# Weight blocks laid side by side for four products, tokens read last to first for two

## The chip, the cores and the metric

The kernel runs on one core of a Trainium2 chip, as one launch. The metric is the device time of that launch in microseconds (us), lower is better; two runs of the kernel before stand at 2233.84 and 2236.26 us, median 2235.05 us. Layouts of the inputs are made on the host ahead of the launch and are not in the time.

## The reference

512 tokens of 1024 features go through two blocks. The first is a gated recurrence and a gated linear attention side by side, then a feed-forward net (FFN 1). The second is a retention layer with FFN 2, then a sparse-attention layer with FFN 3. What matters here are the large products, each a token matrix against a weight matrix:

```python
# first block, D_MODEL = 1024, D_FF = 2816
h = rms_norm(x, norm1[l]);  p = h @ w_in[l]                     # w_in_t (17 tiles), w_in_v
x = x + mix                                                      # mix = ... @ w_out[l]
h = rms_norm(x, norm2[l]);  gate, up = jnp.split(h @ w_ffn_in[l], 2, axis=-1)   # ffn1_in (44 tiles)
x = x + (jax.nn.silu(gate) * up) @ w_ffn_out[l]                  # ffn1_out
return rms_norm(x, final_norm)
...
# second block, for layer 0 (retention) and layer 1 (sparse attention)
normed = rms_norm_2(h, mix_norm_pre[layer])
proj = x @ w_in                       # retention: ret_t (32 tiles), ret_v; attention: kv_t, kv_v, nsa_t
h = h + rms_norm_2(mixed, mix_norm_post[layer])
normed = rms_norm_2(h, ffn_norm_pre[layer])
h = h + rms_norm_2(swiglu_ffn(normed, ffn_w_in[layer], ffn_w_out[layer]), ffn_norm_post[layer])  # ffn2, ffn3
```

The comments name the kernel's own products.

## The kernel before

**Layout.** Activations lie with features on the 128 partitions: XT, AH and AL are [128, 8, 512], eight feature blocks of 512 tokens. A product is computed in tiles of 128 output features by 512 tokens. Each float32 operand is split in two float32r parts, a high one (AH, WH) and the rest (AL, WL), and every block of 128 input features takes three matrix multiplications: high by high, high weight by low activation, low weight by high activation. `part` (matmul line L379) issues one such block. The weight block, 128 x 128, is the stationary operand, which TensorE loads column by column ahead of the multiplication; the activation block, 128 x 512, is the moving operand, which streams through. So each matmul has a weight load of its own, even where the same WH block serves two in a row. A tile of a product with 1024 input features is 8 blocks, 24 loads and 24 matmuls of 512 columns. `tokens` (L427) does the products that are wanted with tokens on partitions; there the activations are the stationary operand and the weights move.

**Weights.** `Plan` lists all weights in the order of use, in units of [128, 1024] (8 blocks of 128 columns, in the host layout made by `feature_tiles`). For each unit SyncE starts one transfer into one of three RAW buffers, ScalarE rounds it into WH (L827), VectorE takes the rest into WL (L1254), and TensorE waits for both. The three buffers of each kind keep this some units ahead. In WH and WL the 128 columns of block k are elements 128 k to 128 k + 127 of each partition: one run.

**Activations.** `high` (ScalarE, L837) writes AH = XT times a gain, `low` (VectorE, L1272) writes AL = XT times the gain less AH. Their key `st` names the product that follows: "a" (w_in), "f1" (FFN 1), "f2", "kv", "q", "f3" (FFN 3); the retention's own are written at L1079 and L1603.

**Order of work.** Every engine has a program written out by hand, with semaphores between them. `three` opens a product: for each feature block as it becomes ready it runs the block of three output tiles, while the norm of the layer before is being applied block by block (for FFN 3: L1585 scale, L1592 add to the stream, L837 high, L1272 low). `fourth` runs the fourth tile with the sums for the norm (L444, L478) in between, `tile` all the others. Results of ffn_in leave PSUM at L1311 with the norm's factor from RS, which has one number for each token, in ascending order of tokens, and the gate (L1040, L1557, L1045, L1559) writes HH and HLO, the operands of ffn_out.

**Strided readers elsewhere.** L1746 copies windows of CK for the attention's compression with an inner step of 16 elements (64 bytes). L1805 adds a bias row read from last to first (inner step of minus one element). L478 spreads one column over 128 (its stationary operand is one column of `rstok`, `rso` or `small`, read 128 times, inner step 0).

Of the kernel before, what the change touches and what calls it, by code (L numbers as in the profile page):

```python
# [10 lines left out]
ACT = mybir.ActivationFunctionType  # L11
ALU = mybir.AluOpType
AX_X = mybir.AxisListType.X

S = 512
# [6 lines left out]
W_SLOTS = 3  # L22
# [11 lines left out]
for _name, _w in VEC_NAMES:  # L34
    VEC_AT[_name] = _n
    _n += _w
NVEC = _n

K_TILES = {"w_in_t": 8, "w_out": 8, "ffn1_in": 8, "ffn1_out": 22, "ret_t": 8, "ret_out": 16, "ffn2_in": 8,
           "ffn2_out": 22, "kv_t": 8, "nsa_t": 8, "nsa_out": 8, "ffn3_in": 8, "ffn3_out": 22}  # L40

# [104 lines left out]
def build(nc, D, out):  # L146
    p = plan()
    n_units = len(p.units)
    with ExitStack() as ctx:
# [6 lines left out]
        XT = sb("XT", [128, 8, S])  # L156
        AH = sb("AH", [128, 8, S], F32R)
        AL = sb("AL", [128, 8, S], F32R)
# [15 lines left out]
        BANK = [ctx.enter_context(nc.psum_tensor(f"bank{i}", [128, 512], F32)) for i in range(8)]  # L174
# [84 lines left out]
        w_high, x_high, squared, rooted = (signal(n) for n in ("w_high", "x_high", "squared", "rooted"))  # L259
        free_a, lru_a, gla_a, gate_a, hid_a, ret_a, kv_a, exped, turned = (  # L260
            signal(n) for n in ("free_a", "lru_a", "gla_a", "gate_a", "hid_a", "ret_a", "kv_a", "exped", "turned"))
        w_low, x_low, added, inverse, stream = (signal(n) for n in ("w_low", "x_low", "added", "inverse", "stream"))
# [13 lines left out]
        def V(name, i=0, n=1):  # L276
            at = VEC_AT[name] + i
            return vec[:, at:at + n]
# [12 lines left out]
        TURN, MIX = 3, 6  # L291
        A_GROUP = len(STEPS) // 4

        def cols(i, br):
            return 7 + 8 * i if br == 0 else 128 * (i + 1)

# [57 lines left out]
        def tensor_program(e):  # L354
            tenant = {}

            def enter(b, key):
# [2 lines left out]
                    e.wait_ge(*freed(tenant[b]))  # L360
                tenant[b] = key

            def part(name, m, kk, x, ready=None, passes=(0, 1, 2)):
                kt, k, u = K_TILES[name], kk % 8, p.first[name, m] + kk // 8
                b, w, sl = p.bank[name, m], u % W_SLOTS, slice(k * 128, (k + 1) * 128)
                for n in passes:
                    if n == 0:
                        if kk == 0:
                            enter(b, (name, m))
                        if k == 0:  # L370
                            e.wait_ge(*w_high.at(u))
                        if ready:
                            e.wait_ge(*ready[0](kk))
                    elif n == 1 and ready:
                        e.wait_ge(*ready[1](kk))
                    elif n == 2 and k == 0:
                        e.wait_ge(*w_low.at(u))
                    wt, xx = (WH[w], x[0]) if n == 0 else (WH[w], x[1]) if n == 1 else (WL[w], x[0])
                    t = e.matmul(BANK[b][:, :], wt[:, sl], xx[:, kk, :], start=kk == 0 and n == 0,  # L379
                                 stop=kk == kt - 1 and n == 2)  # L380
                    if n == 2 and kk == kt - 1:
                        t.then_inc(matmul.did(("unit", u), (name, m)))
                    elif n == 2 and k == 7:
                        t.then_inc(matmul.did(("unit", u)))
# [143 lines left out]
            for f in range(2):  # L528
                enter(6 + f, ("kt", f))
                e.wait_ge(*gla_v.at(("k", f)))  # L530
                for tt in range(4):
                    t = e.transpose(BANK[6 + f][:, ROWS[tt]], KG[:, f, ROWS[tt]], ident[:, :])
# [92 lines left out]
            for h in range(4):  # L625
# [21 lines left out]
                for j in range(4):  # L647
                    n = S - 128 * j
                    b = p.bank["scores", h, j]
# [4 lines left out]
                    for d in range(2):  # L654
                        t = e.matmul(BANK[b][:, 0:n], KR[:, d, j * 128:(j + 1) * 128], QR[:, d, j * 128:S],  # L655
                                     start=d == 0, stop=d == 1)
                    t.then_inc(matmul.did(("scores", h, j)))
                tile("ret_t", 8 * h + 4, A)
                for j in range(4):
                    e.wait_ge(*free_v.at(("scores", h, j)))  # L660
                    e.wait_ge(*free_a.at(("ret_v", h, j)))
                    for et in range(4):
                        if j == 0:
                            enter(4 + et, ("or", h, et))
                        t = e.matmul(BANK[4 + et][:, j * 128:S], VR[:, j, et * 128:(et + 1) * 128], ST[j][:, :],  # L665
                                     start=j == 0, stop=j == 3)
# [61 lines left out]
            for tt in range(4):  # L728
                t = e.transpose(BANK[6][:, 48 * tt:48 * tt + 48], T[3][0:48, ROWS[tt]], ident[0:48, 0:48])
# [66 lines left out]
            for f in range(8):  # L796
                b = 2 + f % 4
# [3 lines left out]
                for i in range(4):  # L801
                    t = e.transpose(BANK[b][:, ROWS[i]], OT[:, i, f * 128:(f + 1) * 128], ident[:, :])
# [12 lines left out]
        def scalar_program(e):  # L815
# [18 lines left out]
                    ahead(p.first[name, c] + q + LOOK)  # L834

            def high(st, f, gain):
                e.activation(AH[:, f, :], XT[:, f, :], ACT.Copy, scale=V(gain, f)).then_inc(x_high.did((st, f)))  # L837

            def square_for_pair(st, f):
                if f > 1:  # L840
# [92 lines left out]
            for f in range(2):  # L933
                e.wait_ge(*gla_v.at(("bc", f)))
                e.activation(DG[:, f, :], BC[:, f, :].rearrange("p (c t) -> p c t", t=64)[:, :, 63], ACT.Exp,
                             scale=1.0 / 16).then_inc(gla_a.did(("decay", f)))
# [12 lines left out]
            for tt in range(4):  # L949
                e.wait_ge(*matmul.at(("w_in_v", 0, tt)))  # L950
                if tt == 0:
                    e.wait_ge(*inverse.at("a"))
                e.activation(VG[:, tt, :], BANK[p.bank["w_in_v", 0, tt]][:, :], ACT.Copy,
                             scale=rstok[:, tt:tt + 1]).then_inc(free_a.did(("w_in_v", 0, tt)))
# [121 lines left out]
            for f in range(8):  # L1076
# [5 lines left out]
                if f > 2:  # L1082
                    e.wait_ge(*added.at(("gained", f - 2)))
                e.activation(SQ2[f % 2][:, :] if f else SUM2[:, :], XT[:, f, :], ACT.Square,
                             scale=V("final_norm", f)).then_inc(squared.did(("gained", f)))
# [158 lines left out]
        def vector_program(e):  # L1244
# [24 lines left out]

            def low(st, f, gain):  # L1270
                e.wait_ge(*x_high.at((st, f)))
                e.scalar_tensor_tensor(AL[:, f, :], XT[:, f, :], V(gain, f), AH[:, f, :], ALU.mult,  # L1272
                                       ALU.subtract).then_inc(x_low.did((st, f)))

            def add_pair(st, q):
                e.wait_ge(*squared.at((st, 2 * q + 1)))
# [640 lines left out]
    return np.ascontiguousarray(w.reshape(k // 128, 128, m // 128, 128).transpose(2, 1, 0, 3).reshape(m // 128, 128, k))  # L1917


def token_tiles(w):  # L1920

    k, m = w.shape
    return np.ascontiguousarray(w.reshape(8, 128, m // 512, 512).transpose(2, 1, 0, 3).reshape(m // 512, 128, 4096))
# [21 lines left out]
def laid_out(inp):  # L1945
# [24 lines left out]
    w = a["w_in"][0]  # L1970
# [27 lines left out]
    w2 = [a[n].reshape(2, 128, 64).transpose(1, 0, 2) for n in ("cmp_w2_k_2", "cmp_w2_v_2")]  # L1998
    w2 = np.stack(w2, axis=1)
    d["cmp_w2"] = np.concatenate([w2, w2], axis=3)  # L2000
    return {k: np.ascontiguousarray(v) for k, v in d.items()}


# [13 lines left out]
```

## Time and profile before

| | |
|---|---|
| runs, median | 2233.84 and 2236.26 us, 2235.05 us |
| profiled execution, own time | 2235.35 us |
| its span, first to last instruction | 2233.6 us |
| mean granted TensorE clock | 0.976 of full |
| PE busy | 2156.9 us, 97% |
| PE weight loads busy | 1774.0 us, 79% |
| VectorE, ScalarE busy | 1043.8 us (47%), 855.1 us (38%) |

PE is TensorE's matmuls, PEld its weight loads, DVE is VectorE, ACT is ScalarE. Matmuls are pipelined: the length of one record (389 ns) reaches over the start of the next, so the busy share says little about the rate, and the distance from one start to the next is the cost of one.

### The profile page before, as it was taken

The numbers are of one execution on the slowest core, as the hardware profiler recorded it, in microseconds if no ns is written. First come the engines' busy times: TensorE is split into PE (matmuls) and PEld (weight loads), VectorE is DVE, ScalarE is ACT, GpSimd is POOL, SyncE is SP. The second block draws the span as 40 slices with busy tenths as digits, with TensorE's granted clock in tenths as the row PEclk, the third lists the DMA queues.
The fourth block names the chain that finished last, engine by engine and source line by source line (L and its number), as shares of the span: only waits on it lengthen the run. The fifth ranks groups of instructions, "written<-read, shape, count | busy, mean of one in ns | idle before, by whom it ended". The sixth has DMA issues, their size and how long they took to land.

```text
span 2233.6 us, 26303 instructions
## 1 busy us (share of the span) xinstructions
PE 2156.9 (97%) x10252; PEld 1774.0 (79%) x10252; DVE 1043.8 (47%) x1939; ACT 855.1 (38%) x1466; POOL 12.7 (1%) x24
## 2 busy tenths in 40 slices
PE   7899999999999999999999999899999999999997
PEld 6677788888878778787888888777888977888886
DVE  5546444434345345334544422564666736444323
ACT  4563333323313323333333322344767744333221
POOL 0000000000000000000000000000000000000000
PEclk9899999999999999999999999999989999999998
DMA  4212333333322222131333333422010022333331
GB/s 132 74 57 76 95 100 98 94 92 93 106 81 77 70 90 85 57 104 57 104 99 100 92 95 93 148 78 85 30 32 18 1 85 66 95 100 98 87 94 64
DMA packets 51818, 184.44 MB, mean 83 GB/s; under 512 B 5818, under 2 KB 6090, under 8 KB 51440
## 3 DMA queue, kind: packets, MB, share of 16 engines
q1 hardware_dynamic: 49248, 171.99, 24.7%
q0 software_dynamic: 2160, 10.63, 1.4%
q8 instruction: 82, 1.34, 0.2%
q14 instruction: 40, 0.33, 0.0%
q10 hardware_dynamic: 288, 0.15, 0.0%
HBM read 180.61 MB, written 2.14 MB: 82 GB/s over the span
## 4 chain that ended last, share of the span: by engine, by line
PE 89%; DVE 5%; ACT 4%; issue 2%; DMA 0%; SPq 0%; DVEq 0%; ACTq 0%
PE bank L379 69%; PE bank L427 6%; PE bank L782 3%; PE bank L762 2%; PE bank L665 1%; DVE WL L1254 1%; PE bank L753 1%; PE bank L776 1%; PE bank L752 1%; PE bank L478 1%; PE bank L655 1%; ACT WH L827 1%; PE bank L444 1%; DVE MF L1585 0%; DMA RAW<-in_w_in_t 0%
## 5 line engine op out<-in xcount | busy, mean ns | idle before, releaser
L379 PE MATMUL bank<-AH,WH 128*128 128x512 f32 x1648 | 654.5, 401 | 22.4 <-ACT AH L837 15.4
L1254 DVE TENSOR_TENSOR WL<-RAW,WH 128x1024 fp32r<-128x1024 f32 (+1 forms) x326 | 391.4, 1205 | 592.9 <-ACT WH L827 592.2
L379 PE MATMUL bank<-AL,WH 128*128 128x512 f32 x1648 | 645.1, 395 | 3.5 <-DVE AL L1272 3.5
L379 PE MATMUL bank<-AH,WL 128*128 128x512 f32 x1648 | 642.2, 394 | 2.4 <-DVE WL L1254 2.4
L827 ACT ACTIVATE WH<-RAW 128x1024 fp32r<-128x1024 f32 (+1 forms) x326 | 338.1, 1041 | 592.4 <-PE bank L379 510.9
L379 PEld LDWEIGHTS bank<-AH,WH 128*128 128x128 f32 x1648 | 313.8, 191 | 93.9 <-issue 20.8
L379 PEld LDWEIGHTS bank<-AL,WH 128*128 128x128 f32 x1648 | 313.6, 191 | 71.9 <-DVE AL L1272 9.7
L379 PEld LDWEIGHTS bank<-AH,WL 128*128 128x128 f32 x1648 | 313.5, 190 | 69.7 <-DVE WL L1254 3.7
L379 PE MATMUL bank<-HH,WL 128*128 128x512 f32 x528 | 208.6, 395 | 0.0
L379 PE MATMUL bank<-HH,WH 128*128 128x512 f32 x528 | 208.6, 395 | 0.0
L379 PE MATMUL bank<-HLO,WH 128*128 128x512 f32 x528 | 208.5, 395 | 0.0
L1311 DVE TENSOR_TENSOR T<-bank,RS 128x512 f32<-128x512 f32 x156 | 106.5, 686 | 162.0 <-PE bank L379 162.0
L379 PEld LDWEIGHTS bank<-HLO,WH 128*128 128x128 f32 x528 | 99.1, 188 | 24.1
L379 PEld LDWEIGHTS bank<-HH,WH 128*128 128x128 f32 x528 | 99.1, 188 | 24.1
L379 PEld LDWEIGHTS bank<-HH,WL 128*128 128x128 f32 x528 | 99.1, 188 | 24.0
L1040 ACT ACTIVATE T<-T 128x512 f32<-128x512 f32 x66 | 41.7, 631 | 127.2 <-DVE T L1311 127.2
L1045 ACT ACTIVATE HH<-T 128x512 fp32r<-128x512 f32 x66 | 41.7, 632 | 125.8 <-DVE T L1557 125.8
L427 PE MATMUL bank<-WH,AH 128*128 128x512 f32 x192 | 77.1, 402 | 5.9 <-DVE XP L1311 3.6
L427 PE MATMUL bank<-WL,AH 128*128 128x512 f32 x192 | 76.9, 401 | 1.6 <-DVE WL L1254 1.6
L427 PE MATMUL bank<-WH,AL 128*128 128x512 f32 x192 | 76.8, 400 | 0.0
L782 PEld LDWEIGHTS bank<-VS,PT 128*128 128x128 f32 x480 | 68.3, 201 | 1.5
L782 PE MATMUL bank<-VS,PT 128*128 128x64 f32 x480 | 68.1, 275 | 0.0
(285 smaller groups left out, 2309.6 us busy)
## 6 DMA issues: line engine op xcount, KB each, us to landing
RAW<-in_ffn_in SPq DMA_DIRECT2D x132, 512.0 KB, 3.5
RAW<-in_ffn_out SPq DMA_DIRECT2D x48, 512.0 KB, 3.5
RAW<-in_ret_t SPq DMA_DIRECT2D x32, 512.0 KB, 3.5
RAW<-in_ffn_out SPq DMA_DIRECT2D x24, 384.0 KB, 3.1
RAW<-in_w_in_t SPq DMA_DIRECT2D x17, 512.0 KB, 3.7
RAW<-in_ret_v SPq DMA_DIRECT2D x16, 512.0 KB, 3.6
RAW<-in_ret_out SPq DMA_DIRECT2D x16, 512.0 KB, 3.6
RAW<-in_nsa_t SPq DMA_DIRECT2D x9, 512.0 KB, 3.5
```

The lines of the kernel that those rows point to most:

```text
L379: t = e.matmul(BANK[b][:, :], wt[:, sl], xx[:, kk, :], start=kk == 0 and n == 0, stop=kk == kt - 1 and n == 2)
L427: t = e.matmul(BANK[b][:, :], xx[:, kk, tt * 128:(tt + 1) * 128], wt[:, sl], start=kk == 0 and n == 0, stop=kk == 7 and n == 2)
L444: t = e.matmul(BANK[4][:, 4 * tt + q:4 * tt + q + 1], SQ[1][:, ROWS[tt]], ones[:, :], start=True, stop=True)
L478: t = e.matmul(BANK[5][:, ROWS[tt]], src[:, at + tt:at + tt + 1].broadcast_to([128, 128]), ident[:, :], start=True, stop=True)
L655: t = e.matmul(BANK[b][:, 0:n], KR[:, d, j * 128:(j + 1) * 128], QR[:, d, j * 128:S], start=d == 0, stop=d == 1)
L762: t = e.transpose(BANK[b][0:k, j * 128:(j + 1) * 128], SS[s % NSS][:, j * 128:j * 128 + k], ident[:, :])
L782: t = e.matmul(BANK[b][:, 64 * br:64 * br + 64], PT[s % NPT][:, j * 128:(j + 1) * 128], VS[:, j, c:c + 64], start=j == 0, stop=j == i)
L827: e.activation(WH[v % W_SLOTS][:, 0:n], RAW[v % RAW_SLOTS][:, 0:n], ACT.Copy).then_inc(w_high.did(v))
L1040: e.activation(a[:, :], a[:, :], ACT.Silu).then_inc(gate_a.did((n, j)))
L1045: e.activation(HH[n][:, j, :], T[2 * (j % 2)][:, :], ACT.Copy).then_inc(hid_a.did((n, j)))
L1254: e.tensor_tensor(WL[w][:, 0:n], RAW[r][:, 0:n], WH[w][:, 0:n], ALU.subtract).then_inc(w_low.did(v))
L1311: e.tensor_tensor(dst, BANK[p.bank[name, m]][:, :], RS[:, :], ALU.mult).then_inc(free_v.did((name, m)))
```

## The change

Two things change, and no instruction is added, removed or moved: on each engine the same operations stand in the same order, on the same tiles, with other access patterns.

**Side by side.** For ffn2_in and ffn3_in two, for ret_t four and for w_in_t eight neighbouring blocks of 128 columns are interleaved column by column on the host (`side_by_side`): column j of the r blocks lie next to each other. The transfer, the rounding (L827) and the remainder (L1254) work on whole units and read and write them in one run as before. The weight load of block k reads 128 elements with a step of r elements, from element (k // r) * 128 r + k % r: steps of 8, 16 and 32 bytes for r = 2, 4 and 8. The other products, ffn1_in among them, keep blocks of one run.

**Backward.** For FFN 1 and FFN 3, `high` writes AH from the last token to the first, `low` reads AH and writes AL that way, and `part` reads AH and AL with an inner step of minus one element as the moving operand of ffn1_in and ffn3_in. Token order in PSUM is as before, so nothing behind it changes.

```diff
+BESIDE = {"ffn2_in": 2, "ffn3_in": 2, "ret_t": 4, "w_in_t": 8}
+BACKWARD = ("f1", "f3")
...
+        def backward(t):
+            return bass.AP(t.tensor, t.offset + S - 1, [t.ap[0], [-1, S]])
+
+        def tokens_of(st, t):
+            return backward(t) if st in BACKWARD else t
...
+            def block(wt, name, k):
+
+                r = BESIDE.get(name, 1)
+                whole = wt[:, :]
+                return bass.AP(whole.tensor, whole.offset + (k // r) * 128 * r + k % r, [whole.ap[0], [r, 128]])
+
             def part(name, m, kk, x, ready=None, passes=(0, 1, 2)):
...
-                b, w, sl = p.bank[name, m], u % W_SLOTS, slice(k * 128, (k + 1) * 128)
+                b, w = p.bank[name, m], u % W_SLOTS
...
-                    t = e.matmul(BANK[b][:, :], wt[:, sl], xx[:, kk, :], start=kk == 0 and n == 0,
+                    t = e.matmul(BANK[b][:, :], block(wt, name, k), backward(xx[:, kk, :]) if name in ("ffn1_in", "ffn3_in") else xx[:, kk, :],
+                                 start=kk == 0 and n == 0,
                                  stop=kk == kt - 1 and n == 2)
...
             def high(st, f, gain):
-                e.activation(AH[:, f, :], XT[:, f, :], ACT.Copy, scale=V(gain, f)).then_inc(x_high.did((st, f)))
+                e.activation(tokens_of(st, AH[:, f, :]), XT[:, f, :], ACT.Copy, scale=V(gain, f)).then_inc(
+                    x_high.did((st, f)))
...
-                e.scalar_tensor_tensor(AL[:, f, :], XT[:, f, :], V(gain, f), AH[:, f, :], ALU.mult,
-                                       ALU.subtract).then_inc(x_low.did((st, f)))
+                e.scalar_tensor_tensor(tokens_of(st, AL[:, f, :]), XT[:, f, :], V(gain, f),
+                                       tokens_of(st, AH[:, f, :]), ALU.mult, ALU.subtract).then_inc(x_low.did((st, f)))
...
+def side_by_side(t, name):
+
+    r = BESIDE[name]
+    m, _, k = t.shape
+    t = t.reshape(m, 128, k // (128 * r), r, 128)
+    return np.ascontiguousarray(t.transpose(0, 1, 2, 4, 3).reshape(m, 128, k))
...
+    for name in BESIDE:
+        d[name] = side_by_side(d[name], name)
```

How many matmuls each part touches (tiles x 8 blocks x 3):

| product | tiles | matmuls | weight step | tokens |
|---|---|---|---|---|
| w_in_t | 17 | 408 | 8 | forward |
| ffn1_in | 44 | 1056 | 1 | backward |
| ret_t | 32 | 768 | 4 | forward |
| ffn2_in | 44 | 1056 | 2 | forward |
| ffn3_in | 44 | 1056 | 2 | backward |

## Rows read from the trace of the kernel before

**Rows 1.** The page: busy time, and the chain that ended last.
```profile
PE 2156.9 (97%) x10252; PEld 1774.0 (79%) x10252; DVE 1043.8 (47%) x1939; ACT 855.1 (38%) x1466; POOL 12.7 (1%) x24
PEclk9899999999999999999999999999989999999998
PE 89%; DVE 5%; ACT 4%; issue 2%; DMA 0%; SPq 0%; DVEq 0%; ACTq 0%
```
**Rows 2.** Busy time of L379 in three stretches: ffn2_in, ffn3_in, ffn1_out.
```profile
core 0: us, PE busy (x) PEld busy (x), PEclk, DMA share, GB/s
1080.00:1280.00 200.00, 200.00 (x884) 165.60 (x883) 1.00 0.31 97
1880.00:2080.00 200.00, 200.00 (x884) 165.62 (x883) 1.00 0.33 98
480.00:600.00 120.00, 120.00 (x516) 96.51 (x515) 1.00 0.33 94
```
**Rows 3.** Timeline in ffn1_in; columns start, length (us), engine, line.
```profile
299.97 0.39 PE L379 MATMUL bank<-AH,WH 128*128 128x512 f32 x1
299.97 0.19 PEld L379 LDWEIGHTS bank<-AL,WH 128*128 128x128 f32 x1
300.20 0.39 PE L379 MATMUL bank<-AL,WH 128*128 128x512 f32 x1
300.20 0.19 PEld L379 LDWEIGHTS bank<-AH,WL 128*128 128x128 f32 x1
300.42 0.39 PE L379 MATMUL bank<-AH,WL 128*128 128x512 f32 x1
```
**Rows 4.** Timeline of PE at half the granted clock, opening of ffn2_in.
```profile
1040.63 0.63 PE L379 MATMUL bank<-AH,WH 128*128 128x512 f32 x1
1041.06 0.63 PE L379 MATMUL bank<-AL,WH 128*128 128x512 f32 x1
1041.49 0.63 PE L379 MATMUL bank<-AH,WL 128*128 128x512 f32 x1
```
**Rows 5.** Short matmuls back to back: busy time of L699 (124 columns each).
```profile
1516.00:1520.00 4.00, 4.00 (x38) 4.00 (x37) 1.00 0.43 133
```
**Rows 6.** Timeline where the next load is L478's, one column read 128 times.
```profile
933.66 0.39 PE L379 MATMUL bank<-AH,WH 128*128 128x512 f32 x1
933.89 0.39 PE L379 MATMUL bank<-AL,WH 128*128 128x512 f32 x1
934.12 0.39 PE L379 MATMUL bank<-AH,WL 128*128 128x512 f32 x1
934.12 0.75 PEld L478 LDWEIGHTS bank<-ident,rso 128*128 128x128 f32 x5
934.34 0.61 PE L478 MATMUL bank<-ident,rso 128*128 128x128 f32 x4
```
**Rows 7.** Groups by shape on VectorE and ScalarE.
```profile
L1272 DVE SCALAR_TENSOR_TENSOR AL<-XT,vec,AH 128x512 fp32r<-128x512 f32 x48 | 35.3, 747 | 13.5 <-ACT AH L837 12.7
L837 ACT ACTIVATE AH<-XT,vec 128x512 fp32r<-128x512 f32 x48 | 33.7, 717 | 40.5 <-DVE XT L1592 25.5 <-DVE XT L1523 14.6
L1805 DVE CUSTOM_DVE_ANT_0 SQ<-bank,TT 128x512 f32<-128x512 f32 x32 | 22.1, 691 | 15.0 <-PE bank L753 14.9
L1746 DVE COPY X<-CK 64x496 f32<-64x496 f32 x16 | 9.8, 612 | 1.0 <-PE bank L699 0.5
L1305 DVE COPY RS<-bank 128x512 f32<-128x512 f32 x5 | 3.5, 691 | 13.5 <-PE bank L478 13.5
```
**Rows 8.** The chain that ended last, in time, at the opening of FFN 3.
```profile
1841.38 0.70 DVE XT L1592
1842.08 0.02 issue
1842.11 0.73 ACT AH L837
...
1853.16 0.67 DVE AL L1272
...
1858.82 0.67 DVE AL L1272
```

## What I expect, written before the changed kernel ran

> **What bounds the kernel now.** I read the page first. TensorE is busy for 97% of the span and makes up 89% of the chain that ended last [rows 1]: the time is, nearly all of it, the number of matmuls times the distance between their starts. Nothing in this change alters the number. So the one question is whether a weight load that reads with a step, or a moving operand read from its end, changes that distance, and everything else is small.
>
> So the second view is the busy time by stretch, used as a counter. In ffn2_in 884 matmuls of 512 columns fit in 200 us, and as many in ffn3_in: 200 / 884 = 0.2262 us each (up to two that reach over the edges are counted too; less those it is 200 / 882 = 0.2267) [rows 2]. In ffn1_out the same shape takes 120 / 516 = 0.2326 us. The granted clock is full, 2.4 GHz, in all three stretches. 512 columns at one column a cycle are 213.3 ns at that clock, so 13.3 ns of each distance, 6%, are something else. ffn1_out differs from the ffn_in products only in where its operands lie (HH and HLO for AH and AL), yet pays 6.4 ns more: where the operands lie can be felt, at the size of a few nanoseconds.
>
> The third view is the timeline. Each weight load starts with the matmul before it and is recorded for 0.19 us, inside the 0.227 us of that matmul: it is hidden [rows 3]. At the half clock (1.2 GHz) the same matmuls start 0.43 us apart, which is 512 columns at 1.2 GHz and nothing over [rows 4]. So the 13 ns are not a fixed price of a matmul; they appear only where columns are asked for at 2.4 GHz. That looks like a limit of what the operand memory delivers, and it is the reason to take the change seriously: an access pattern is what such a limit would depend on.
>
> **The change, part by part.**
>
> *Loads with a step: 2112 matmuls with step 2 (ffn2_in, ffn3_in), 768 with step 4 (ret_t), 408 with step 8 (w_in_t); 3288 in all.* No row of this trace shows a strided weight load. I bound it by neighbours.
>
> How much longer may a load get before anyone notices? L699's matmuls are short (124 columns, 0.05 us of streaming at full clock for each pass), so there loads follow one another as fast as they can: 38 loads and matmuls touch a stretch of 4 us, and with some two cut at the edges that is 4.0 / 36 = 0.111 us from one to the next [rows 5]. That is the true occupancy of a load; the recorded 0.19 us holds its latency too. Against a distance of 0.2267 us the cover is 0.115 us: a load may take twice as long (0.222 us) and still be hidden, by 4 ns.
>
> Does a step slow a reader at this pace? A load takes 128 columns in 0.111 us, 0.87 ns each. The nearest rows are VectorE's. The copy L1746 reads with a step of 64 bytes, twice the largest step of the change: 496 elements in 612 ns. The plain copy L1305 takes 691 ns for 512. Per element that is 1.23 and 1.35 ns, so the strided one pays nothing that one can see [rows 7]. VectorE is another reader, but its pace (about 1 ns an element) is close to a load's. So I take 0 for the length of the load, with the cover as a second reason.
>
> Does a load with a step disturb the stream beside it? From below: where the load beside the stream reads one single column 128 times (L478), the smallest stretch of memory a load can touch, the next start still comes 0.22 us after (934.12 to 934.34), the same as between plain ones [rows 6]. So a load that touches less gives nothing back, and the 13 ns are not paid for the memory that a load touches. That speaks for 0 also where it touches more. The bounds stay wide. Above: ffn1_out's 6.4 ns for operands that lie less well, times 3288 = +21 us. Below: the floor of 213.3 ns, -13.4 x 3288 = -44 us, if the new pattern freed the stream altogether, for which no row speaks. I take 0.
>
> The Trainium skill has a rule against this part. "SBUF — State Buffer", section "SBUF: two separate sides", says that the memory has lines of 16 bytes and that at least two successive accesses to a line are needed for full bandwidth; "Advanced Engine Details and Errata", section "Memory Cachelines", says the same. By it step 2 (8 bytes, two columns a line) is free and steps 4 and 8 (one column a line) are penalised, and the backward read (four tokens a line) is free. The row of L1746, with one element a line and no penalty, disagrees for VectorE. By the rule taken as a doubling of 1176 loads the sum would still be 0, since twice 0.111 us is hidden.
>
> *Backward moving operand: 2112 matmuls (ffn1_in, ffn3_in).* No row shows TensorE reading backward. L1805 on VectorE reads its second operand with a step of minus one: 691 ns for 512 columns, as the forward copy [rows 7]. So direction costs nothing there. But TensorE reads 2.4 elements a nanosecond, over twice VectorE's rate, so the row decides less here than I would like. Above: if reading backward held the stream to half pace, the distance would be that of the half clock, 0.4267 us [rows 4]. Nearer above: 6.4 ns x 2112 = +14 us, the price of place. Below: -13.4 x 2112 = -28 us. I take 0, the row of the only backward reader.
>
> *ScalarE and VectorE: 16 writes of AH and 16 of AL (717 and 747 ns each) turn backward.* [rows 7] For FFN 1 they lie behind a tile of w_out each (24 matmuls, 5.4 us), which hides even a doubling. For FFN 3 the opening chain runs through one L837 and two L1272 (0.73, 0.67, 0.67 us) [rows 8]: 0 if backward writes go at the old pace, +2.1 us if each doubles. L1805 says 0. The rounding of weights (L827, L1254) and the transfers work on runs as before: 0.
>
> **The sum.** 0 + 0 + 0 against the profiled execution's own 2235.35 us, which lies 0.3 us over the median of the runs. I forecast 2236 us, no change. The terms' own bounds near the rows (+21, +14, +2) reach 2272; below I leave some 13 us for a part of the stream's surplus. A measurement of this kernel tells about 2% (45 us) from no change.
>
> **The rivals.**
>
> *1. The stepped load takes from the stream (slower, 12%).* Suppose the surplus of 13.3 ns is the load's reading from the same memory as the stream after all, and grows with the stretch over which the 128 columns are spread: two, four and eight times 13.3 ns. Then +13.3 ns x 2112 = +28 us, +40 x 768 = +31 us, +93 x 408 = +38 us: +97 us, 2332 us. It decides (passes 2%) when it is about half as strong. For it: the surplus exists, it vanishes at the half clock, and it moves with the place of the operands. Against it: the one-column load of rows 6, which touches the least and saves nothing. By the Trainium skill's 16-byte line ("SBUF — State Buffer", as above) the growth would end at step 4, since a column then has a line to itself; the sum by it would be +28 +31 +16 = +75 us, an estimate.
>
> *2. The backward stream runs at half pace (slower, 10%).* A reader that must deliver 2.4 elements a nanosecond may do it by fetching ascending neighbours together. Backward it would fall to one at a time: (0.4267 - 0.2267) x 2112 = +422 us, 2658 us; a loss of 10% of the pace is enough to pass 2% (0.0227 x 2112 = 48 us). For it: the stream is the one reader here that is already at a limit. Against: L1805. The skill's rule, with four accesses to a line either way, sides against this rival too; no run so far shows it.
>
> *3. The load outgrows its cover (slower, 6%).* If steps 4 and 8 make a load three times as long (0.333 us), the load becomes the bound in ret_t and w_in_t: (0.333 - 0.2267) x 1176 = +125 us, 2360 us; four times, (0.444 - 0.2267) x 1176 = +256 us. It decides where a load passes twice its length. This is the direction of the skill's rule, and L1746 is against it.
>
> *4. The new patterns lift the surplus (faster, 4%).* The distance falls to 213.3 ns wherever a pattern changes: 4344 matmuls (3288 + 1056 of ffn1_in) x 13.4 ns = -58 us, 2177 us. For it is only that ffn1_in and ffn1_out differ by place. For a gain of over 2% three quarters of it must come.
>
> That the change does not do what it says I give nothing: host layout and read pattern fit together, and the engines' programs are the same in order and tiles.
>
> **How the numbers follow.** No effect 68%, rivals 12, 10, 6 and 4%. The predicted time is that of no effect, 2236 us; its own range is 2222 to 2272. To hold eight in ten the range goes on to rival 1 with its upper end, 2335 us; rivals 2 to 4 (20%) stay outside. Slower by over 2% is 12 + 10 + 6 = 28%, faster 4%, within 2% 68%.
>
> **What would show it.** In the profile after, the same count over 1080 to 1280 us shows step 2 alone; ffn1_in shows direction alone; ffn3_in shows both; ret_t step 4; w_in_t step 8, in the stretches between its waits. 0.2267 in all five proves the forecast; a longer distance in ffn1_in proves rival 2, one that grows from ffn2_in to ret_t to w_in_t rival 1; matmuls that begin to wait for loads, with weight loads recorded for 0.3 us or more and only in ret_t and w_in_t, rival 3. Loads recorded for longer than 0.19 us with the distance kept would show that a step costs and the cover holds. L837 and L1272 at 717 and 747 ns test the small term. What would make me wrong is, most of all, that VectorE's rows don't carry over to a reader at 2.4 elements a nanosecond.

## The result, and the profile of the changed kernel

The changed kernel takes 2268.6 us (2266.74 and 2270.46), against 2235.05 us: a ratio of 1.0147, 95% interval 1.0122 to 1.0171. It is slower by 33.5 us, clear of the scatter and inside 2%. The profiled execution is the one of 2270.46 us, its span 2268.7 us.

The page of the changed kernel, for [rows 1]. The lines of the code have moved by 16 to 18 (`part` is L395, L444 is `tokens`, L854 is `high`, L1290 is `low`).

```profile
PE 2193.8 (97%) x10252; PEld 1852.9 (82%) x10252; DVE 1043.9 (46%) x1939; ACT 854.8 (38%) x1466; POOL 12.7 (1%) x24
PEclk9889999999999999999999999999989999999998
PE 90%; DVE 5%; ACT 3%; issue 1%; DMA 0%; SPq 0%; DVEq 0%; ACTq 0%
```

VectorE and ScalarE have the same busy time to 0.3 us. Weight loads have 79 us more. The chain that ended last is TensorE's as before.

Where the time went shows best when both profiles are cut at the same places in the work. First the kernel before, then the changed one: the opening with w_in and w_out, ffn1_in, the retention, ffn2_in, ffn3_in. Columns: stretch, its length, busy time and count for each engine (PE, PEld, DVE, ACT, POOL), granted clock as a share of full, DMA share, GB/s.

```profile
0.00:231.00 231.00, 206.46 (x957) 163.12 (x958) 124.35 (x197) 118.23 (x151) 4.28 (x10) 0.96 0.27 86
231.00:477.00 246.00, 243.41 (x1082) 200.75 (x1081) 110.88 (x134) 77.36 (x92) 0.00 (x0) 1.00 0.31 96
...
600.00:940.50 340.50, 338.19 (x1493) 269.67 (x1492) 144.38 (x199) 109.21 (x142) 3.81 (x7) 0.98 0.25 79
...
1038.90:1287.40 248.50, 247.28 (x1096) 203.71 (x1097) 124.50 (x156) 83.39 (x103) 0.00 (x0) 0.99 0.29 91
...
1843.00:2092.00 249.00, 247.83 (x1096) 204.08 (x1097) 124.45 (x156) 83.34 (x103) 0.00 (x0) 0.99 0.30 90
```

```profile
0.00:240.30 240.30, 216.00 (x957) 188.19 (x958) 124.55 (x197) 118.23 (x151) 4.29 (x10) 0.94 0.25 83
240.30:492.70 252.40, 249.86 (x1081) 200.82 (x1080) 110.81 (x133) 77.21 (x92) 0.00 (x0) 1.00 0.29 94
...
615.40:963.00 347.60, 346.23 (x1494) 306.42 (x1493) 144.82 (x199) 109.25 (x142) 3.81 (x7) 0.98 0.23 78
...
1061.30:1316.30 255.00, 253.95 (x1096) 209.34 (x1097) 124.43 (x156) 83.31 (x103) 0.00 (x0) 0.99 0.28 89
...
1872.10:2127.90 255.80, 254.82 (x1096) 213.86 (x1097) 124.44 (x156) 83.38 (x103) 0.00 (x0) 0.99 0.27 88
```

The differences are +9.3 us (opening, steps of 8), +6.4 (ffn1_in, backward), +7.1 (retention, steps of 4), +6.5 (ffn2_in, steps of 2) and +6.8 (ffn3_in, both), 36.1 in all. The stretches in between give back 1.0, and the span is 35.1 us longer. So each touched stretch pays 6.4 to 9.3 us, for quite different edits and for 408 to 1056 touched matmuls.

The opening also ran longer at the half clock: its granted clock is 0.94 for 0.96, and of its 408 w_in_t matmuls 31 start 426 or 427 ns after the one before, where 20 did in the kernel before. Eleven matmuls at 427 ns in place of 245 are 2.0 us of its 9.3, an estimate from these starts. The run of the steps alone (below) shows 0.94 in its opening as well. Why the clock stayed low for longer there is not shown.

The count of matmuls by stretch, for [rows 2]: ffn1_in, ffn2_in, ffn3_in, ffn1_out, and 30 us of ret_t; the first and the last hold a wait each.

```profile
260.00:460.00 200.00, 197.43 (x844) 158.36 (x844) 1.00 0.30 98
1100.00:1300.00 200.00, 200.00 (x858) 165.42 (x858) 1.00 0.30 97
1920.00:2120.00 200.00, 200.00 (x859) 168.86 (x858) 1.00 0.28 93
500.00:600.00 100.00, 100.00 (x432) 81.09 (x431) 1.00 0.30 93
870.00:900.00 30.00, 29.35 (x125) 29.06 (x125) 1.00 0.29 97
```

200 us hold 858 matmuls where they held 884: 0.2333 us from start to start, for 0.2267. From here on, a distance is the mean time from the start of one matmul to the next, at full clock and without waits (under 0.26 us), over a whole product of the profiled execution. ffn1_in, ffn2_in and ffn3_in are at 233.3 to 233.4 ns, ret_t at 235.3 ns, w_in_t at 244.7 ns (before 226.8 to 226.9, then 227.5 and 227.8, which have short stretches between waits). The three ffn_out products, which were not touched, went from 233.3 to 232.4 ns.

The loads themselves, from the view of one source line, in ffn2_in (step 2), ffn3_in (step 2, backward stream), ret_t (step 4), w_in_t (step 8) and ffn1_in (step 1); the three numbers are the shortest, the middle and the longest in ns.

```profile
L395 PEld LDWEIGHTS bank<-AH,WH x286: 193/193/193, 1099.8 to 1299.3; 128*128 128x128 f32 x143
...
L395 PEld LDWEIGHTS bank<-AH,WH x286: 197/197/197, 1919.9 to 2119.4; 128*128 128x128 f32 x143
...
L395 PEld LDWEIGHTS bank<-AH,WL x42: 308/310/311, 869.8 to 899.7; 128*128 128x128 f32 x42
...
L395 PEld LDWEIGHTS bank<-AL,WH x24: 315/331/342, 39.9 to 59.1; 128*128 128x128 f32 x24
...
L395 PEld LDWEIGHTS bank<-AL,WH x282: 188/188/192, 263.3 to 459.9; 128*128 128x128 f32 x141
```

The recorded load takes 188 ns for one run, 193 to 197 for step 2, 310 for step 4, 331 for step 8. The jump, 113 to 117 ns, lies between a step of 8 bytes and one of 16.

And where no stream of 512 columns runs ahead of a load, the longer load shows at once. The timeline of the changed kernel after L495 (the short matmuls of the norm), in ret_t:

```profile
703.71 0.94 PE L495 MATMUL bank<-ident,rso 128*128 128x128 f32 x7
704.41 0.60 PE L395 MATMUL bank<-AH,WH 128*128 128x512 f32 x1
704.86 0.40 PE L395 MATMUL bank<-AL,WH 128*128 128x512 f32 x1
705.09 0.40 PE L395 MATMUL bank<-AH,WL 128*128 128x512 f32 x1
```

The second L395 starts 0.45 us after the first. The same place before (timeline of PE in the kernel before):

```profile
689.05 0.48 PE L379 MATMUL bank<-AH,WH 128*128 128x512 f32 x1
689.37 0.39 PE L379 MATMUL bank<-AL,WH 128*128 128x512 f32 x1
```

There it was 0.32 us. The 0.13 us more are about the growth of the recorded load, 310 ns for 188.

### The profile page after: what moved, and what is told of

Its sections match the earlier page's. It is cut to its first block, busy times and chain, and to the rows that moved or that the text cites. A ratio compares the mean times of both kernels' runs of the same rounds, so it can differ in the third digit from the quotient of the medians.

```text
span 2268.7 us, 26303 instructions
## 1 busy us (share of the span) xinstructions
PE 2193.8 (97%) x10252; PEld 1852.9 (82%) x10252; DVE 1043.9 (46%) x1939; ACT 854.8 (38%) x1466; POOL 12.7 (1%) x24
## 4 chain that ended last, share of the span: by engine, by line
PE 90%; DVE 5%; ACT 3%; issue 1%; DMA 0%; SPq 0%; DVEq 0%; ACTq 0%
PE bank L395 71%; PE bank L444 6%; PE bank L799 3%; PE bank L779 2%; PE bank L682 1%; PE bank L770 1%; DVE WL L1272 1%; PE bank L793 1%; PE bank L769 1%; PE bank L495 1%; PE bank L672 1%; ACT WH L844 1%; PE bank L461 1%; PE bank L578 0%; DMA RAW<-in_w_in_t 0%
## 5 line engine op out<-in xcount | busy, mean ns | idle before, releaser
L395 PE MATMUL bank<-AH,WH 128*128 128x512 f32 x1648 | 671.0, 411 | 22.7 <-ACT AH L854 16.6
L395 PE MATMUL bank<-AL,WH 128*128 128x512 f32 x1648 | 658.6, 403 | 3.0 <-DVE AL L1290 2.9
L395 PE MATMUL bank<-AH,WL 128*128 128x512 f32 x1648 | 654.9, 402 | 0.9 <-DVE WL L1272 0.9
L395 PEld LDWEIGHTS bank<-AH,WH 128*128 128x128 f32 x1648 | 366.3, 223 | 82.7 <-issue 20.3
L395 PEld LDWEIGHTS bank<-AL,WH 128*128 128x128 f32 x1648 | 367.1, 223 | 59.4 <-DVE AL L1290 9.3
L395 PEld LDWEIGHTS bank<-AH,WL 128*128 128x128 f32 x1648 | 366.8, 223 | 54.6 <-DVE WL L1272 1.8
L395 PE MATMUL bank<-HH,WL 128*128 128x512 f32 x528 | 208.3, 395 | 0.0
L395 PE MATMUL bank<-HH,WH 128*128 128x512 f32 x528 | 208.3, 395 | 0.0
L395 PE MATMUL bank<-HLO,WH 128*128 128x512 f32 x528 | 208.3, 395 | 0.0
L395 PEld LDWEIGHTS bank<-HH,WL 128*128 128x128 f32 x528 | 99.5, 188 | 23.3
L395 PEld LDWEIGHTS bank<-HH,WH 128*128 128x128 f32 x528 | 99.5, 188 | 23.2
L395 PEld LDWEIGHTS bank<-HLO,WH 128*128 128x128 f32 x528 | 99.5, 188 | 23.1
L444 PE MATMUL bank<-WH,AH 128*128 128x512 f32 x192 | 76.9, 401 | 6.6 <-DVE XP L1329 4.4
L444 PE MATMUL bank<-WL,AH 128*128 128x512 f32 x192 | 76.5, 398 | 1.6 <-DVE WL L1272 1.6
L444 PE MATMUL bank<-WH,AL 128*128 128x512 f32 x192 | 76.3, 397 | 0.0
```

The lines of the kernel that those rows point to most:

```text
L395: t = e.matmul(BANK[b][:, :], block(wt, name, k), backward(xx[:, kk, :]) if name in ("ffn1_in", "ffn3_in") else xx[:, kk, :], start=kk == ...
L444: t = e.matmul(BANK[b][:, :], xx[:, kk, tt * 128:(tt + 1) * 128], wt[:, sl], start=kk == 0 and n == 0, stop=kk == 7 and n == 2)
```

## The experiments

After the first look two theories stood. **Meeting:** TensorE's stream and the load beside it read the same memory, and the distance depends on how the two walks through it meet, which is place, step and direction together; on top of that a step of 16 bytes or more makes the load itself long. **Pattern price:** each departure from a forward run has its fixed price, wherever the operands lie.

**Steps moved to other products.**

```diff
-BESIDE = {"ffn2_in": 2, "ffn3_in": 2, "ret_t": 4, "w_in_t": 8}
-BACKWARD = ("f1", "f3")
+BESIDE = {"ffn1_in": 4, "ffn2_in": 8, "ffn3_in": 4, "ret_t": 2}
+BACKWARD = ("f3",)
```

> The steps change places among the products: step 4 for ffn1_in (forward), step 8 for ffn2_in (forward), step 4 with backward tokens for ffn3_in, step 2 for ret_t, plain w_in_t. If the step sets the load and the distance, whatever the product: ffn1_in loads 310 ns and a distance of 235 to 236.5 ns, ffn2_in loads 329 ns and 244.7 ns, ret_t loads 193 ns and 233.3 ns, w_in_t 226.7 ns between its waits; about +45 us in all, 2280 us. If instead the longer distances of ret_t and w_in_t in the changed kernel came from what runs between their tiles, ffn1_in and ffn2_in stay at 233.3 ns and the total is some 2262 us.

Measured: 2283.62 us, the kernel before 2231.16 beside it. From the starts: ffn1_in (step 4) 235.05 ns with loads of 310 ns; ffn2_in (step 8) 244.2 ns, loads 329; ffn3_in (step 4, backward) 233.3 ns, loads 311; ret_t (step 2) 234.3 ns, loads 196; w_in_t plain 228.0 ns. The windows by stage:

```profile
270.00:470.00 200.00, 200.00 (x853) 200.00 (x853) 1.00 0.31 95
1090.00:1290.00 200.00, 200.00 (x821) 200.00 (x821) 1.00 0.30 92
1920.00:2120.00 200.00, 200.00 (x859) 200.00 (x859) 1.00 0.30 96
```

The recorded load follows the step, in whatever product; the distance follows it to within 2 ns. The load unit (second busy column) is now busy for all 200 us. With steps of 4, backward reading is no dearer than forward; it is even 1.7 ns cheaper (ffn3_in against ffn1_in), so the step alone does not fix the distance.

**One address.**

```diff
+        def one_token(t):
+            return bass.AP(t.tensor, t.offset, [t.ap[0], [0, S]])
...
+                if name in ("ffn1_in", "ffn3_in"):
+                    whole = wt[:, :]
+                    return bass.AP(whole.tensor, whole.offset + k * 128, [whole.ap[0], [0, 128]])
```

`one_token` is the moving operand of ffn2_in; BESIDE is empty, BACKWARD holds "f3" alone, and ffn3_in alone reads backward.

> Parts of the products are left out: the loads of ffn1_in and ffn3_in read one column 128 times, the stream of ffn2_in reads one token 512 times; ffn3_in's stream is backward. If the surplus over 213.3 ns is a meeting of load and stream in memory, a load that stays at one address changes it in ffn1_in (towards 213 ns, or to another value than 226.7), and ffn3_in is no longer at 233.3 ns. If it belongs to the stream alone, ffn1_in stays at 226.7, ffn3_in at 233.3 ns, and ffn2_in, whose stream stays at one address, falls towards 213 to 216 ns.

```profile
260.00:460.00 200.00, 199.74 (x864) 162.52 (x865) 1.00 0.32 100
1070.00:1270.00 200.00, 200.00 (x929) 175.25 (x928) 1.00 0.33 104
1870.00:2070.00 200.00, 200.00 (x859) 160.93 (x858) 1.00 0.32 98
```

2229.53 us. ffn2_in, whose stream stays at one token, is at 215.9 ns with plain loads beside it: of the surplus over 213.3 ns only 2.6 ns are left, so plain loads cost such a stream no more than that. ffn1_in, whose loads stay at one column, is at 231.1 ns, worse than the 226.7 of plain ones: a load can disturb a walking stream by where it reads, and touching less memory does not help on average. (Split by pass, the distance is 225.8 ns where the load beside the stream reads the same column as the load before it, and 233.4 and 234.2 ns beside the two others.) ffn3_in with a backward stream stays at 233.3 ns even so. Neither expectation is met whole. The surplus needs a walking stream (so far the stream's own), and its size depends on the load (so far the meeting).

**Place of the stream.** The kernel before with pads, such as

```diff
+            sb("pad_1", [128, 96], stack=ar)
             HH[1] = sb("HH1", [128, 22, S], F32R, ar)
```

and the same ahead of MH (96 elements), RH (32), HH of FFN 2 (16) and of FFN 3 (8).

> The kernel before, with the moving operands of the later products put elsewhere by pads: HH of FFN 1 and MH 384 bytes on (the same place modulo 512 bytes as AH and the weights), RH 128 bytes on, HH of FFN 2 64 and of FFN 3 32 bytes on. If place relative to the weights sets the distance: ffn1_out falls from 233.3 to 226.7 ns, and ret_out does too if the period is 256 bytes; the other two take other values. About -4 to -14 us. If the 233.3 ns of ffn1_out belongs to the product (22 blocks, other readers beside it), nothing moves.

The windows are ffn1_out, ret_out, ffn2_out and ffn3_out:

```profile
490.00:590.00 100.00, 100.00 (x443) 82.78 (x442) 1.00 0.33 96
940.00:1010.00 70.00, 70.00 (x310) 57.99 (x309) 1.00 0.32 105
1290.00:1390.00 100.00, 100.00 (x430) 80.17 (x429) 1.00 0.32 93
2090.00:2190.00 100.00, 100.00 (x428) 80.39 (x428) 1.00 0.30 87
```

2225.37 us for 2231.16 (one execution each). ffn1_out and ret_out fell from 233.3 to 226.67 ns, w_out from 232.6 to 227.2; HH of FFN 2, moved by 64 bytes, stayed at 233.3 and that of FFN 3, moved by 32, went to 234.3 ns. RH was moved by 128 bytes and HH of FFN 1 by 384, with the same result; so the place seems to count modulo 256 bytes, as far as these two places tell. With all weight buffers at one place modulo 512 bytes, good is where the stream begins at the same place, and bad are 128, 160 and 192 bytes beyond it. The ffn_out and ret_out products were not slow by themselves; their operands lay badly.

**Place of the weights.** The kernel before, with gaps between the weight buffers, so that the WH begin 0, 32 and 64 and the WL 128, 256 and 384 bytes off, modulo 512.

> The kernel before, with the six weight buffers at six different places modulo 512 bytes (WH 0, 32, 64 and WL 128, 256, 384 bytes from where they were), AH and AL unmoved. If load and stream meet by relative place, the distance in ffn1_in differs by buffer, between 213 and 240 ns, with WH0 at 226.7. If only the stream's own place counts, all six stay at 226.7 ns and the total at 2235 us.

```profile
270.00:470.00 200.00, 200.00 (x865) 162.62 (x864) 1.00 0.32 98
```

2260.01 us with not one access pattern changed: 29 us more than the one execution beside it, which had a granted clock of 0.979 for 0.975, and 25 us more in span than the profile of the kernel before, with 0.976. The distances account for some 21 us (an estimate: their growth times the matmuls of each product). ffn1_in is at 231.6 ns; by the buffer that is being loaded, from the starts: WH0 230.6, WH1 233.5, WH2 231.9, WL0 232.5, WL1 231.2, WL2 228.6. WH0, not moved and expected at 226.7, rose as well: its second load in a row is at 227.2 ns, but its first, which follows one of a WL, at 233.9. So the load before leaves its mark too. No rule of one buffer's place comes out of this: WL1, 256 bytes off, is at 231.2 ns, not at 226.7, and WL2, 384 off, is the best of the WL. The stream's place alone is refuted: it was the same throughout. What ScalarE and VectorE write into these buffers moved along with them, and this run does not separate it from the loads; only the one-address run changed the loads alone.

**Activations moved, in the changed kernel.**

```diff
+        sb("pad_a", [128, 32])
         AH = sb("AH", [128, 8, S], F32R)
         AL = sb("AL", [128, 8, S], F32R)
+        sb("pad_b", [128, 96])
```

> The changed kernel with AH and AL 128 bytes further on, the weights where they were modulo 512 bytes. If the 233.3 ns of ffn1_in, ffn2_in and ffn3_in are a fixed price of a step or of a direction, all three stay. If they are the price of how load and stream meet, they move: ffn1_in, where both now walk downwards, could go to 226.7 ns or away from it, and the plain products (kv_t, nsa_out, at 226.7 so far) rise to 233.3 as HH did at that place. Loads stay at 188, 193, 310 and 329 ns under either.

```profile
280.00:480.00 200.00, 200.00 (x846) 158.73 (x845) 1.00 0.31 95
1100.00:1300.00 200.00, 200.00 (x866) 169.09 (x865) 1.00 0.31 99
1920.00:2120.00 200.00, 200.00 (x859) 167.14 (x858) 1.00 0.31 95
```

2274.84 us. ffn1_in (backward) rose from 233.3 to 236.4 ns, ffn2_in (step 2) fell from 233.3 to 231.4, ffn3_in (both) stayed at 233.3, and the plain nsa_out rose from 227.0 to 233.0. A fixed price of the pattern is refuted for the first two.

ret_t bears on the loads: its step, its weights' place and its recorded loads (309 to 311 ns) are those of the changed kernel, yet its distance rose from 235.3 to 239.4 ns. Two stretches of ret_t without a wait, the changed kernel first:

```profile
873.00:900.00 27.00, 27.00 (x117) 27.00 (x117) 1.00 0.28 91
...
881.00:908.00 27.00, 27.00 (x114) 27.00 (x114) 1.00 0.29 86
```

So where the loads are long, the place of the stream still counts.

**Six places, three steps, all backward.** BESIDE is 2 for ffn2_in and ret_t, 4 for ffn3_in; all three ffn_in are backward; the weight buffers lie 32 bytes apart.

> All three ffn_in products backward, with steps 1, 2 and 4 (ffn1, ffn2, ffn3), ret_t step 2 forward, w_in_t plain, and the six weight buffers 32 bytes apart in place modulo 256. If load and stream meet by relative place, the distance differs by buffer; in ffn2_in, where load (two columns' worth of bytes in two cycles) and backward stream walk the same way at the same pace, they could keep clear of each other at some places: distances down to 216 ns there, and above 233 at others. If the price is fixed by pattern, all buffers stand at 233.3 in the three products.

```profile
270.00:470.00 200.00, 200.00 (x859) 161.12 (x858) 1.00 0.31 97
1090.00:1290.00 200.00, 200.00 (x859) 166.68 (x858) 1.00 0.31 96
```

2260.62 us. The hope for 216 ns was wrong: ffn2_in is at 233.3 at every one of the six places, ffn3_in as well, and ffn1_in between 232.2 (WH0) and 236.0 (WL0). With a backward stream 233.3 ns is what comes nearly everywhere; no buffer under a backward stream averaged below 232, whereas forward 226.7 is to be had. Of the two theories the pattern price is refuted and the meeting fits what was seen, but it is no more than a frame: its forecasts of single distances (226.7 for WH0, 216 here) failed.

**All streams in the good place.** The kernel before with pads of 96 elements ahead of MH, RH and the three HH.

> The kernel before with five pads of 384 bytes, so that MH, RH and all HH and HLO lie at the same place modulo 256 bytes as the weights; nothing else differs. If the finding of the placed streams holds, w_out, ffn1_out, ret_out, ffn2_out and ffn3_out stand at 226.7 ns: 2160 matmuls x 6.7 ns = -14 us, about 2220 us, a ratio of 0.9937 to before. If place matters only in the profile and not in the time, the ratio is 1.

2218.47 us against 2237.68 (5 and 8 executions), ratio 0.9924, interval 0.9900 to 0.9947. ffn1_out, ret_out, ffn2_out and ffn3_out are all at 226.67 ns:

```profile
490.00:590.00 100.00, 100.00 (x443) 82.81 (x442) 1.00 0.34 96
...
1290.00:1390.00 100.00, 100.00 (x443) 82.81 (x442) 1.00 0.33 98
2100.00:2200.00 100.00, 100.00 (x443) 82.81 (x442) 1.00 0.29 87
```

Expected were 14 us and a ratio of 0.9937, which lies within the interval; the measured ratio makes 17 us. The profiled execution is one of 2229.7 us at a mean granted clock of 0.972, the five reach from 2215.63 us (0.979) to 2229.70, so its rows serve for the distances and not for the total. This version beats both kernels.

**Each part alone.** First all blocks in one run again (`BESIDE = {}`).

> The changed kernel with all weight blocks in one run again: the backward tokens alone. From the profile of the changed kernel, 2112 matmuls (ffn1_in, ffn3_in) at 233.3 ns for 226.7: +14 us, ratio 1.0063. If the backward writes of ScalarE and VectorE cost as well, up to 2 us more. If the two parts simply add up in ffn3_in, this kernel and the next together give the whole +33.5 us; if ffn3_in pays the 6.7 ns once, they give 7 us more than the whole.

2246.43 against 2235.94 us: ratio 1.0050, 1.0032 to 1.0068, where 1.0063 was expected. ffn1_in and ffn3_in are at 233.3 ns, ffn2_in at 226.9. Then `BACKWARD = ()` and the plain `xx[:, kk, :]` as moving operand.

> The changed kernel with forward tokens: the stepped weight loads alone. ffn2_in and ffn3_in at 233.3 ns (+14 us), ret_t at 235.3 (+7 us), w_in_t at 244.7 ns and its uncovered loads (+9 us): +30 us less 1 us in the ffn_out products, ratio 1.013. If the steps were free in time and only the backward reading cost, the ratio would be 1.00.

2263.47 us: ratio 1.0127, 1.0093 to 1.0161, where 1.013 was expected. ffn2_in and ffn3_in 233.25 ns, ret_t 235.4, w_in_t 244.7, ffn1_in 226.8. The intervals do not decide whether the parts add. The distances do: ffn3_in pays some 6.5 ns over its 226.9 with either part alone (233.35 and 233.25) and with both (233.4). They do not add.

**Streams too short to cover a load.**

```diff
+                    whole = name not in ("ffn1_in", "ffn2_in", "ffn3_in", "ret_t") or (kk, n) in ((0, 0), (kt - 1, 2))
+                    c = slice(0, 512 if whole else 256)
+                    t = e.matmul(BANK[b][:, c], block(wt, name, k), xx[:, kk, c], start=kk == 0 and n == 0,
```

> Forward tokens. In ffn1_in (step 8), ffn2_in (step 4), ffn3_in (step 2) and ret_t (plain) all matmuls of a tile but the first and the last stream 256 of the 512 columns: half of the product is left out, so that the stream (107 ns) no longer covers a load. The distance then shows how long a load holds its place. If the recorded load grows by what its place grows: 111 ns plain and some 113 ns in ret_t, 115 to 118 ns with step 2, 111 + 122 = 233 ns with step 4, 111 + 141 = 252 ns with step 8. If the growth is mostly latency and the loads still follow each other at 111 ns, all four products stand at 113 to 125 ns.

The timelines of PE: ffn2_in (step 4), then ffn3_in (step 2).

```profile
1150.15 0.40 PE L397 MATMUL bank<-AL,WH 128*128 128x256 f32 x1
1150.38 0.40 PE L397 MATMUL bank<-AH,WL 128*128 128x256 f32 x1
1150.62 0.40 PE L397 MATMUL bank<-AH,WH 128*128 128x256 f32 x1
...
1950.14 0.28 PE L397 MATMUL bank<-AH,WL 128*128 128x256 f32 x1
1950.26 0.28 PE L397 MATMUL bank<-AH,WH 128*128 128x256 f32 x1
1950.38 0.28 PE L397 MATMUL bank<-AL,WH 128*128 128x256 f32 x1
```

2149.94 us, with half of four products left out. Half the columns stream, and with step 4 the distance is still 0.233 us, with step 8 (ffn1_in) 235 to 245 ns, 241 on average; with step 2 and plain it is 0.12 us. So a load holds its place for at most 120 ns with steps 1 and 2 (there the stream's 107 ns may be the bound), for 233 ns with step 4 and for some 241 ns with step 8. In the changed kernel ret_t (235.3 ns) and w_in_t (244.7 ns) stand 2 and 4 ns above these values: the load has become the larger bound there. It is not the only one, since ret_t went to 239.4 ns with the activations moved.

## Why the prediction was right, and where it was not

**Right:** within 2%, inside the range, and the number of matmuls times their distance as what counts. Nothing on ScalarE and VectorE: L854 takes 717 ns and L1290 748, against 717 and 747 in [rows 7], and the backward ones among them, before and after, 724.0 and 724.2 (FFN 1, high), 719.9 and 720.6 (FFN 3, high), 751.2 and 752.0, 746.0 and 746.6 (low). A weight load's place of 0.111 us [rows 5] is not contradicted: the short streams bound it at 0.12 us.

That the forecast of no effect came out inside 2% is in part luck. Its own range, 2222 to 2272 us, held only through the bounds from neighbours (+21, +14, +2 us); every zero on TensorE was wrong, all in the same direction, and the steps of 4 and 8 happened to reach just past the cover. At three times the load, rival 3's own price was +125 us.

**Wrong:** the sum. I forecast 2236 us, no effect; 33.5 us came, with an interval of 27 to 38 us. Three zeros fell: the length of the load, the stream beside a stepped load, and the backward stream.

*"I take 0 for the length of the load"* [rows 7]. Recorded loads took 193 to 197, 310 and 331 ns for 188. The row of VectorE's strided copy did not carry over to TensorE. The rule of the Trainium skill ("SBUF — State Buffer", "SBUF: two separate sides": lines of 16 bytes, two accesses to each wanted), which I set against that row, is what TensorE's loads followed: step 2 holds the place no longer than 0.12 us, step 4 doubles it to 0.233. The measurement agrees with the rule for TensorE's loads. Between steps 4 and 8 the runs show some 8 ns more, of which the rule says nothing.

*"Twice 0.111 us is hidden, by 4 ns."* It was 2.1 and 2.2 times, 233 and 241 ns, against 226.7. That is rival 3, the load that outgrows its cover, which I had priced from three times on (+125 us) and given 6%. Its mechanism is shown by the short streams, for the same steps in ffn2_in and ffn1_in; its size in ret_t and w_in_t is at most the +7.1 and +9.3 us of their stretches. Both hold the uncovered loads behind waits and norms (some 0.12 us each), the latter also the 2.0 us of the clock, and I had counted neither.

*"Does a load with a step disturb the stream? I take 0."* Step 2 costs 6.6 ns a matmul where the load is hidden: 6.5 us in ffn2_in. I had argued from L478 in [rows 6] that a load that touches less gives nothing back, so one that touches more takes nothing. A load at one address cost 4.4 ns in ffn1_in. The row had one such load in it, beside streams that already stood at 226.7 ns, the best of the forward streams here; it could not show what a worse pattern takes away. Rival 1, growth with the spread, is refuted: it wanted 240, 267 and 320 ns for steps 2, 4 and 8, and 233.3, 235.3 and 244.7 came. Rival 4 did not come either: no touched product fell.

*"Backward: I take 0, the row of the only backward reader"* [rows 7]. 6.6 ns x 2112 = 14 us, the "nearer above" bound, which was taken from ffn1_out [rows 2], also at 233.3 ns. The run with the streams placed shows that ffn1_out pays for place; that direction is the same effect is suggested by the equal size and not shown. I had that row before me, as a sign that place is felt, and used it for a bound only. In ffn3_in it did not add to the step's. Rival 2 (half pace, 426.7 ns) is refuted.

So the sum: 7.0 (ffn1_in) + 7.0 (ffn2_in) + 7.0 (ffn3_in), from 6.6 ns times 1056 matmuls each, + 7.1 (retention) + 9.3 (opening), both as their stretches were measured and not worked out from parts, - 1.5 (1584 matmuls of ffn_out that lost 0.9 ns) = 36 us, for 35.1 us of span.

**Open:** how the memory is built, such that place and direction matter, and whether 256 bytes is the period: the moved streams fit it, the six moved weight buffers follow no such rule. Between 226.7 ns and the 215.9 ns of a stream at one address lie 10.8 ns a matmul, 77 us over 7104 of them. None of the placements tried reached below 226.7 on average, and no theory here says whether one can. Nor is it explained why untouched ffn_out products changed by 0.9 ns; they follow products whose distances changed, but so does ret_out, which stayed at 233.3. And it is open why step 4 stands at 233, 235 or 239 ns with loads of the same recorded length.

## What to carry to other kernels

Read the distance between starts, product by product, and compare it with columns over granted clock: two products of one shape that differ by 3% may have their operands in different places, and a pad of a few hundred bytes may be all the repair (here 0.8% of the kernel). Keep float32 weight blocks in one run: a step of 16 bytes or more doubled the load's place (233 ns and more), and a cover of 512 streamed columns (227 ns) was just too short for that. A row of one engine is a weak witness for another: VectorE's rows failed for the stream, which reads at more than twice its rate, and for the load, whose rate is near its own. Give such a zero a wide bound on the side the mechanism points to.

## What the runs showed of the hardware that I had not expected

- The same matmul (512 float32r columns, full clock) starts 215.9 ns after the one before with a stream at one address, 226.7 ns in the best placed walk, 233.3 to 234.3 ns in a badly placed one, 233.3 in most backward ones, 236.4 ns in the worst arrangement tried without long loads.
- Moving six weight buffers by 0 to 384 bytes, and nothing else, cost some 21 us by the distances (25 to 29 us in the time, about 1%, one execution); moving five activation tiles to the right place gains 0.76%.
- A load of 128 float32r columns holds its place for up to 0.12 us with columns 4 or 8 bytes apart, 233 ns at 16 bytes, some 241 ns at 32 bytes.
- ScalarE's backward writes, and VectorE's backward reads and writes, cost less than 1 ns in 720 to 752.
